# Where the split operands of three feed-forwards lie within 512 bytes of SBUF

## The reference

```python
def swiglu(x, w_gate, w_up, w_down):
    return (jax.nn.silu(x @ w_gate) * (x @ w_up)) @ w_down
...
def conv_ffn(h, w_up, conv_w, w_down):
    a, g = jnp.split(dwconv(h @ w_up, conv_w), 2, axis=-1)
    return (jax.nn.silu(g) * a) @ w_down
```

## The kernel before

| products | w_hi | w_lo | x_hi | x_lo |
|---|---|---|---|---|
| feed-forward 1, before | 448 | 0 | 384 | 0 |
| feed-forwards 2 and 3, before, gate and up | 448 | 0 | 384 | 256 |
| feed-forward 2, before, down | 448 | 0 | 384 | 0 |
| feed-forward 3, before, down | 448 | 0 | 384 | 256 |
| first mixer (`late_parts`, `u_parts`) | 448 | 0 | 128 | 0 |
| second mixer (`scratch_parts`, `u_parts`) | 448 or 192 | 0 | 384 | 0 |
| its branches (`branch_parts`, `branch_uppers`) | 0 | 0 | 192 | 192 |
| its output, first two tiles | 0 | 0 | 128 | 0 |
| its output, last six tiles | 448 | 0 | 128 | 0 |

## Time and profile before

### The profile page before, as it was taken

How to read it: one execution, slowest core, us unless ns; L and a number is a source line. 1 busy time by engine, 2 the same in 40 slices (tenths; PEclk the granted TensorE clock), 3 DMA queues, 4 the chain that set the end, 5 groups by cost and what they waited for, 6 DMA issues and landing times.

```text
span 1206.9 us, 24404 instructions
## 1 busy us (share of the span) xinstructions
PE 1178.4 (98%) x9128; PEld 1111.1 (92%) x9128; DVE 816.0 (68%) x1121; ACT 637.3 (53%) x1018; POOL 527.1 (44%) x285
## 2 busy tenths in 40 slices
PE   6999999999999999999999999999999999999998
PEld 6999999987889899999999879987877999999998
DVE  7788875856865577777654852688836596655555
ACT  6444446525762555454546546468517635655553
POOL 0343436732465533343436645458530483232331
PEclk9999998999999999999989999999999999999999
DMA  6888884543334467878614333233323254666663
GB/s 221 277 278 294 283 280 130 190 140 123 105 108 137 157 210 259 292 274 292 188 52 158 123 99 129 88 106 105 105 70 106 88 175 140 208 185 188 188 189 121
DMA packets 58100, 207.10 MB, mean 172 GB/s; under 512 B 6576, under 2 KB 8240, under 8 KB 57776
## 3 DMA queue, kind: packets, MB, share of 16 engines
q1 hardware_dynamic: 49824, 177.23, 45.2%
q0 software_dynamic: 6912, 25.17, 5.7%
q10 hardware_dynamic: 1296, 3.74, 0.9%
HBM read 205.07 MB, written 1.05 MB: 171 GB/s over the span
## 4 chain that ended last, share of the span: by engine, by line
PE 82%; DVE 8%; issue 3%; ACT 3%; POOL 2%; DMA 1%; DVEq 0%; SPq 0%; POOLq 0%; ACTq 0%
PE psum L641 23%; PE psum L642 23%; PE psum L643 22%; POOL own_parts L2944 2%; PE psum L789 1%; PE psum L1017 1%; PE psum L942 1%; PE psum L652 1%; PE psum L654 1%; PE psum L653 1%; PE psum L666 1%; PE psum L1346 1%; POOL high L3039 1%; DVE u_parts L2882 1%; PE psum L700 1%
## 5 line engine op out<-in xcount | busy, mean ns | idle before, releaser
L641 PE MATMUL psum<-parts 128*128 128x256 f32 x1584 | 441.0, 278 | 14.0 <-DVE parts L2197 10.4
L642 PE MATMUL psum<-parts 128*128 128x256 f32 x1584 | 445.7, 281 | 0.0
L643 PE MATMUL psum<-parts 128*128 128x256 f32 x1584 | 441.6, 279 | 0.0
L641 PEld LDWEIGHTS psum<-parts 128*128 128x128 f32 x1584 | 299.5, 189 | 14.9 <-issue 11.0
L2952 POOL TENSOR_TENSOR parts<-low,parts 128x1024 fp32r<-128x1024 f32 x60 | 151.0, 2517 | 367.4 <-ACT parts L1520 367.4
L643 PEld LDWEIGHTS psum<-parts 128*128 128x128 f32 x1584 | 299.7, 189 | 0.0
L642 PEld LDWEIGHTS psum<-parts 128*128 128x128 f32 x1584 | 299.7, 189 | 0.0
L1520 ACT ACTIVATE parts<-low 128x1024 fp32r<-128x1024 f32 x198 | 207.4, 1056 | 163.1 <-DMA low<-stream 162.4
L2944 POOL TENSOR_TENSOR own_parts<-low,parts 128x1024 fp32r<-128x1024 f32 x75 | 184.9, 2479 | 151.5 <-ACT parts L1598 147.4
L2197 DVE TENSOR_TENSOR parts<-low,parts 128x1024 fp32r<-128x1024 f32 x138 | 163.6, 1219 | 23.6 <-ACT parts L1520 22.9
L642 PE MATMUL psum<-u_parts,parts 128*128 128x256 f32 (+1 forms) x560 | 164.7, 294 | 0.0
(11 more groups left out here) (384 smaller groups left out, 2091.1 us busy)
## 6 DMA issues: line engine op xcount, KB each, us to landing
low<-stream SPq DMA_DIRECT2D x334, 512.0 KB, 3.6
high<-conditioning POOLq DMA_DIRECT2D x48, 512.0 KB, 5.0
high<-wuq ACTq DMA_DIRECT2D x1, 1152.0 KB, 5.1
low<-x SPq DMA_DIRECT2D x4, 256.0 KB, 6.3
high<-ctx ACTq DMA_DIRECT2D x1, 1024.0 KB, 6.4
out<-low SPq DMA_DIRECT2D x8, 128.0 KB, 1.8
low<-cst ACTq DMA_DIRECT2D x1, 850.5 KB, 4.8
low<-vec ACTq DMA_DIRECT2D x1, 157.5 KB, 6.3
```

Of the source, the lines that this page charges most:

```text
L641: pe.matmul(out, w_hi[:, cols_], x_hi, start=start, stop=False, **kw)
L642: pe.matmul(out, w_hi[:, cols_], x_lo, start=False, stop=False, **kw)
L643: return pe.matmul(out, w_lo[:, cols_], x_hi, start=False, stop=stop, **kw)
```

## The change

Only the table of starts is changed. No instruction is added or removed, and no array changes its size. The three starts of `ring_lo` go to 0. The four starts of the activations' parts become one number in each feed-forward.

```diff
-PART_STARTS = ({"ring_lo": 16, "u_hi": 112, "u_lo": 16, "hidden_hi": 112, "hidden_lo": 144},
-               {"ring_lo": 16, "u_hi": 112, "u_lo": 80, "hidden_hi": 112, "hidden_lo": 144},
-               {"ring_lo": 16, "u_hi": 112, "u_lo": 80, "hidden_hi": 112, "hidden_lo": 208})
+PART_STARTS = ({"u_hi": 96, "u_lo": 96, "hidden_hi": 96, "hidden_lo": 96},
+               {"u_hi": 64, "u_lo": 64, "hidden_hi": 64, "hidden_lo": 64},
+               {"u_hi": 16, "u_lo": 16, "hidden_hi": 16, "hidden_lo": 16})
```

## The result

The changed kernel takes 1221.09 us (median of 6 runs, 1218.12 to 1223.20), the kernel before 1210.33 us in its 6 runs. The ratio is 1.0091, with a 95% interval of 1.0065 to 1.0116. So it is slower by 0.9%, some 11 us. The profiled span is 1218.1 us, 11.2 above that of before.

A forecast was written before the change was run, and what follows sets the result against it. The prediction took TensorE's distance between matmul starts in the feed-forwards as the bound; +10.4 us on the 1206.9 us span gave 1217.3, and 1.4 us from span to median gave 1218.7, range 1201 to 1229.

The forecast's parts named there:

- What bounds the kernel: Inside each feed-forward TensorE never waits, so time is the number of matmuls times the distance between two starts.
- Slower, on the path, with no cover: In the feed-forwards all the added matmul time, +10.4 us, reaches the total, since TensorE waits nowhere inside them.
- The price of 6.6 ns for each product: In all three feed-forwards a product of three matmuls goes from 346.6 to 353.2 ns, +10.4 us over 1584 products.
- the third rival: Equal places meet at every matmul: 120.0 ns in feed-forwards 1 and 2, +17.8 us together, 1226 us; chance 20%.
- x342: Matmul count forecast for a 40 us stretch inside each feed-forward, instead of x349, with three equal durations of 281 ns.
- The total: Whole kernel: +10.4 us on the profiled span gives 1217.3, plus 1.4 for the median of the runs, 1218.7 us; chance 38%.
- the structure that the change brings: The mixers' branches, weights' parts at 0 and activations' at 192, 117.7 ns per matmul, taken as the feed-forwards' new price.
- the mixers' rows must stay as they are: Sign expected in the profile after: matmul rates in the mixers, branches included at 117.7 ns, do not change.
- Equality or place: Dear matmuls (117.7 to 120.0 ns) come from equal weights' places modulo 512, or upper weights at a multiple of 128 bytes.
- L642 as the dear one of three: In a feed-forward product L642, beside which the block at 0 is loaded, is slowest: 280 ns, 4 over L641.
- second rival: Places do not matter; busier VectorE and GpSimd make the mixers' rows dear; nothing changes, 1208.3 us; chance 12%.
- the rule set against the whole sum: Skill text giving TensorE a second independent read port for weight loads, so two places never meet and the time stays.

## Why the prediction was right, step by step

**What bounds the kernel: right.** TensorE is busy for all of each window, before and after, and the time followed the distance between two starts.

**Slower, on the path, with no cover: right.** 14.7 us of longer feed-forwards, and none of it hidden by the waits.

**The price of 6.6 ns for each product: right for feed-forward 3, too small for the others.** The forecast took 117.7 ns everywhere. Measured are 118.7, 120.0 and 117.8. Feed-forward 2 at a distance of 256 got the price of `stay_awake`, which the third rival had given to both of the first two. The sum over the feed-forwards is 14.7 us instead of 10.4. Of the signs named ahead, x342 came in feed-forward 3 alone; the first two have x339 and x336, and 384 bytes, a distance that the trace didn't have, costs neither 117.7 nor 120.0.

**The total: right by an offset.** The prediction had no term for the clock. In the profiles the part that was too small was made up by 3.3 us between feed-forwards 2 and 3, almost all of it the stretch of half clock that the first profile of before had. In the timed runs the changed kernel's higher mean clock gives back some 2.2 us (the estimate above). That the two errors met is luck, and the forecast of 1218.7 against 1221.09 is closer than its terms. Against the 1210.33 us of the kernel before over 6 runs, the measured difference is 10.8 us, and 10.4 was forecast.

**The branches as "the structure that the change brings": the step that doesn't carry.** They were priced from one stretch of one profile. The same code at the same places ran at 113.3 ns in the profile of the changed kernel, and twelve matmuls of the branches in the profile of before did so too. So a distance of 192 has two rates, and the row showed one. The sign "the mixers' rows must stay as they are" failed by this, without the forecast being wrong for it. That feed-forward 3 came out at its 117.8 is no confirmation of the row. At the distance of 64 only 117.8 was seen, in three profiles.

**Equality or place: neither.** The prediction couldn't tell equal places of the weights from places at a multiple of 128 bytes. The move by 64 bytes left all three rates, so place by itself isn't the cause. The activations moved alone show that the equality of the weights' places isn't needed for the loss.

**L642 as the dear one of three: right row, wrong reading.** L642 has the longest distance to the next start, 118.3 ns. But with its stream moved to an odd multiple of 64 it became dearer, 121, and drew the other two along. The three numbers of a product aren't prices that can be changed one by one.

**No change, with VectorE and GpSimd in the mixers as the cause of the dear rows (second rival): out.** The time rose by 10.8 us, and so the rule set against the whole sum, by which it would stay, fails here too. In the branches of the changed kernel GpSimd is busy for 16.00 of 16 us, and the matmuls take 113.3 ns.

## What to carry to other kernels

Where TensorE never waits, its rate can still differ by 6% (113.3 to 120.0 ns for the same 128x256 matmul), by how the SBUF addresses of blocks and streams lie to one another. At two of the distances tried it even differs with the same addresses. Count matmuls in a window and compare with columns over clock before looking for other waste. Before taking a price from a row of the same kernel, see whether other stretches with the same operands, or another profile, show the same price. And a term that is confirmed by a total needs its own row: here a too small term and an unforeseen gain of the clock met in the sum.

## What the runs showed of the hardware

**The rates are few.** Over 14 profiles the feed-forwards ran at 113.3, 115.6, 117.8, 118.5, 118.7 or 120.0 ns for each matmul. For a product of three these are 340, 346.7, 353.3, 356 and 360 ns, but for the one at 118.5, which was seen once. With one column in each cycle, as the half-clock stretch shows, 256 columns at 2.4 GHz are 106.7 ns, 320 for three; 16 columns are 6.67 ns. So a product takes its columns and 3, 4, 5, 5.4 or 6 times 16 columns more: one or two such steps for each matmul. 16 columns of 4 bytes are 64 bytes. That the step is one group of 64 bytes in which stream and load meet is an argument from these numbers and wasn't tested.

**With all parts of the weights at one place, and all of the activations at another,** the rates by distance were:

| distance in bytes | ns for each matmul, with the number of feed-forwards seen |
|---|---|
| 0 | 120.0 (1) |
| 256 | 120.0 (3) |
| 128 | 118.7 (1) |
| 384 | 118.7 (2) |
| 64 | 117.8 (3) |
| 320 | 117.8 (1) |
| 192 | 117.8 (4), 113.3 (1), both in one (1) |
| 448 | 113.3 (2), 117.8 (1) |

The branches, also at 192, had 117.8 in their stretch of 228 matmuls in twelve profiles and 113.3 in two. All of it is consistent with a period of 256 bytes. A rate, once taken, lasted for a whole feed-forward, unless a gap or the extra matmul of 64 columns came between. What decides at the start which of two rates is taken stays open.

**The arrangement of before** (distances 448, then 0 or 256, then 448) gave 115.6 ns in all thirteen feed-forwards that had it, in five kernels, also behind an extra matmul. Its worth is not that it has the best rate but that it has one.
